# A hybrid diffusion step on one core: the first layer's v split into bf16 halves during the mixer, its expert output in three bf16 passes

## What is computed

```python
def _peer(x, w_q, sub_keys, u, v):
    ...
    best, pos = lax.top_k(cand, PEER_TOPK)
    eidx = jnp.take_along_axis(cidx, pos, axis=-1)
    gate = jax.nn.softmax(best, axis=-1)
    ...
    def block(args):
        xb, ib, gb = args
        hb = jax.nn.gelu(jnp.einsum('tkd,td->tk', u[ib], xb), approximate=False)
        return jnp.einsum('tk,tkd->td', gb * hb, v[ib])
```

## Time and profile before

| | us |
|---|---|
| median of 3 runs | 4829.14 (4827.85 to 4833.03) |
| the profiled execution | 4834.75, its span 4833.2 |
| PE busy | 4347.5 (90%) |
| DVE busy | 3212.7 (66%) |
| ACT busy | 1013.2 (21%) |
| POOL busy | 720.5 (15%) |
| DMA | 1101.75 MB, mean 228 GB/s |

### The profile page before, as it was taken

One profiled execution on the slowest core, in us unless ns is written; L12 is line 12 of the kernel. 1 busy time (PEld: TensorE's weight loads), 2 busy tenths in 40 slices (PEclk: granted clock), 3 DMA queues, 4 the chain that ended last, 5 costly groups with the idle time before them and its releaser, 6 DMA issues. The chain is left out here.

```text
span 4833.2 us, 54964 instructions
## 1 busy us (share of the span) xinstructions
PE 4347.5 (90%) x19374; PEld 2496.9 (52%) x19374; DVE 3212.7 (66%) x6400; ACT 1013.2 (21%) x1581; POOL 720.5 (15%) x548
## 2 busy tenths in 40 slices
PE   8999998978979989999998877987878998999998
PEld 5767674645545545544444555554444554444443
DVE  1666642679978767765653675469997886766664
ACT  2111101122224431100001253213333441100000
POOL 0000000002221113232210000001221112332220
PEclk9999999989989999999999999999998999999999
DMA  4111131149877779999992000116776779999995
GB/s 146 39 39 44 37 133 55 55 182 350 324 278 267 294 275 375 370 385 394 384 360 70 31 1 31 47 50 242 282 284 234 284 272 353 364 397 400 400 396 196
DMA packets 291813, 1101.75 MB, mean 228 GB/s; under 512 B 30704, under 2 KB 131184, under 8 KB 222576
## 3 DMA queue, kind: packets, MB, share of 16 engines
q0 software_dynamic: 74752, 539.00, 28.3%
q1 hardware_dynamic: 185136, 470.64, 27.2%
q10 hardware_dynamic: 31680, 88.88, 4.8%
HBM read 1005.61 MB, written 92.80 MB: 227 GB/s over the span
## 5 line engine op out<-in xcount | busy, mean ns | idle before, releaser
L774 POOL DMA_INDIRECT room_p<-in_uv,ga_eidx_p x512 | 702.8, 1373 | 3309.5 <-DVEq L801 2105.0
L1324 PE MATMUL ex_psF_p<-ex_vst_p,ex_gh_p 128*128 128x512 f32 x1920 | 851.5, 599 | 34.3 <-DVE ex_gh_p L1405 18.1
L800 DVE SCALAR_TENSOR_TENSOR ga_acc_p<-room_p,ga_gw_p,ga_acc_p 128x1024 f32<-128x1024 f32 x504 | 625.1, 1282 | 21.8 <-issue 1.7
L1324 PEld LDWEIGHTS ex_psF_p<-ex_vst_p,ex_gh_p 128*128 128x128 f32 x1920 | 365.9, 192 | 482.5 <-issue 460.6
L786 DVE CUSTOM_DVE_ANT_0 room_p<-room_p,hx_p 128x1024 f32<-128x1024 f32 x512 | 605.5, 1220 | 4.0 <-issue 4.0
L891 PE MATMUL eh_psH_sl_p<-h_hi_p,eh_uhi_sl_p 128*128 128x384 bf16 x1056 | 367.6, 348 | 160.0 <-DVE eh_ulo_sl_p L855 159.9
L1324 PE MATMUL ex_psF_p<-ex_ust_p,ex_gh_p 128*128 128x512 f32 x1152 | 502.1, 593 | 6.6 <-DVE ex_gh_p L1405 6.5
L1405 DVE TENSOR_TENSOR ex_gh_p<-ex_est_p,ex_gst_p 128x384 f32<-128x384 f32 x196 | 107.3, 558 | 397.7 <-DMA ex_est_p<-hidden 253.3
L891 PE MATMUL eh_psH_sl_p<-h_lo_p,eh_uhi_sl_p 128*128 128x384 bf16 x1056 | 366.3, 347 | 0.0
L1324 PEld LDWEIGHTS ex_psF_p<-ex_ust_p,ex_gh_p 128*128 128x128 f32 x1152 | 217.7, 190 | 286.6 <-issue 285.4
L891 PE MATMUL eh_psH_sl_p<-h_hi_p,eh_ulo_sl_p 128*128 128x384 bf16 x1056 | 365.4, 346 | 0.0
(11 more groups left out here) (248 smaller groups left out, 6275.5 us busy)
## 6 DMA issues: line engine op xcount, KB each, us to landing
ex_vst_p<-in_uv SPq DMA_DIRECT2D x160, 512.0 KB, 8.4
eh_ust_sl_p<-in_uT SPq DMA_DIRECT2D x132, 512.0 KB, 5.4
gates<-gt_gs_p ACTq DMA_DIRECT2D x24, 2048.0 KB, 8.0
ex_gst_p<-gates SPq DMA_DIRECT2D x128, 384.0 KB, 13.0
ex_ust_p<-in_uv SPq DMA_DIRECT2D x96, 512.0 KB, 9.3
ex_est_p<-hidden SPq DMA_DIRECT2D x196, 192.0 KB, 10.2
eh_ust_gt_p<-in_uT SPq DMA_DIRECT2D x64, 512.0 KB, 6.6
ex_ust_p<-in_uT SPq DMA_DIRECT2D x60, 512.0 KB, 8.8
```

What stands on the lines that cost most here:

```text
L774: self.nc.gpsimd.indirect_dma_start(self.slot[s % self.RING], None, self.uv, bass.IndirectOffsetOnAxis(self.eidx[:, s:s + 1], 0)).then_inc ...
L800: nc.vector.scalar_tensor_tensor(acc[:], row, self.gw[:, s:s + 1], acc[:], op0=ALU.mult, op1=ALU.add)
L1324: last = nc.tensor.matmul(psF[:, t, x, :], gh[n % 3][:, P * t:P * t + P], vbuf[vslot[n]][:, BANK * x:BANK * x + BANK], start=(n == 0), sto ...
```

## The change

During the first layer's mixer, v of all 128 steps is brought in, split and written back: POOL fetches 128 rows x 1024 fp32 (512 KB) into one of two slots, ACT rounds them to bf16 (`high`), DVE subtracts (`low`) to get the bf16 remainder, and POOL stores both halves (512 KB) to a DRAM tensor `halves`. There are 16 such tiles in each of the 8 heads; the two slots of raw rows and of halves are handed back through POOL. In the expert stage of the first layer v is then loaded from `halves`, as many bytes as before, and `output` makes three bf16 passes, high·high, low·high and high·low, of 6 matmuls each. The gated values are split for it: ACT rounds gh(n), DVE subtracts, in the early steps in the same step, behind u's low half, in the later ones a step behind. gh(n) now waits for the split of gh(n-3), and four buffers of halves wait for the output. The second layer's expert stage is untouched. Two tensors of 2 partitions share one buffer to make room.

```diff
@@ rec_mixer
+            def fetch(h, j):
+                pool.dma_start(vraw[j % 2][:], rows_in[h, j, :, D:2 * D]).then_inc(v_in[j % 2], 16)
+            def stored(h, j):
+                pool.wait_ge(v_out[j % 2], 16 * (VSPLIT // 2 * h + j // 2) + 16)
+                pool.sem_inc(v_free, 1)
+            def split_rows(h, nxt):
+                for j in range(VSPLIT):
+                    pool.wait_ge(v_low, VSPLIT * h + j + 1)
+                    pool.dma_start(halves[h, j], vhl[j % 2][:]).then_inc(v_out[j % 2], 16)
+                    if j + 2 < VSPLIT:
+                        fetch(h, j + 2)
+                    elif nxt is not None:
+                        fetch(nxt, j + 2 - VSPLIT)
+                    if j > 0:
+                        stored(h, j - 1)
+                stored(h, VSPLIT - 1)
             load(0)
+            fetch(0, 0)
+            fetch(0, 1)
             with pool.Fori(1, RH) as h:
+                split_rows(h - 1, h)
                 store(h - 1)
...
+            def high(h, js):
+                for j in js:
+                    act.wait_ge(v_in[j % 2], 16 * (VSPLIT // 2 * h + j // 2) + 16)
+                    act.wait_ge(v_free, VSPLIT * h + j + 1)
+                    nc.scalar.activation(vhl[j % 2][:, 0, :], vraw[j % 2][:], ACT.Copy).then_inc(v_high, 1)
...
-                evacuate(h, s, [Q_, FF_, FB_, G_])
+                for n in (Q_, FF_, FB_, G_):
+                    high(h - 1, range(VSPLIT * n // 4, VSPLIT * (n + 1) // 4))
+                    evacuate(h, s, [n])
...
             for g in range(later.groups):
+                high(RH - 1, range(VSPLIT * g // later.groups, VSPLIT * (g + 1) // later.groups))
...
+            def low(h, n):
+                for j in range(VSPLIT * (n - 1) // 16, VSPLIT * n // 16):
+                    dve.wait_ge(v_high, VSPLIT * h + j + 1)
+                    nc.vector.tensor_tensor(vhl[j % 2][:, 1, :], vraw[j % 2][:], vhl[j % 2][:, 0, :],
+                                            ALU.subtract).then_inc(v_low, 1)
...
                     build(h, s, n)
                     take(h, n - 1)
+                    low(h, n)
...
                 for d in range(2):
+                    low(h, 15 + d)
                     n = TR0 + d
@@ peer_experts
+                    sp.dma_start(vbuf[vslot[n]].bitcast(BF16), halves[n]).then_inc(v_in[vslot[n]], 16)
...
+                for t in range(ND):
+                    tok = slice(P * t, P * t + P)
+                    for j, (g, v0) in enumerate(((g_hi[n % GH], 0), (g_hi[n % GH], D), (g_lo[n % GH], 0))):
+                        for x in range(2):
+                            last = nc.tensor.matmul(psF[:, t, x, :], g[:, tok], both[:, v0 + BANK * x:v0 + BANK * x + BANK],
+                                                    start=(n == 0 and j == 0), stop=(n == NK - 1 and j == 2))
...
             for n in range(NK):
+                if halves is not None:
+                    high(n)
                 gelu(n + 1)
                 take_u(n + 3)
...
                 if n >= 3:
-                    dve.wait_ge(added, n - 2)
+                    dve.wait_ge(added if halves is None else g_low, n - 2)
...
                 take_u(n + 3)
+                while halves is not None and lows < (n + 1 if n < late or n == NK - 1 else n):
+                    low(lows)
+                    lows += 1
                 while gather.paired < begun + paired(n):
```

More of the change, by code:

```diff
@@ L222, in rec_mixer @@
         adab = sb("rec_adab", [P, NMOD * KD, 2])
-        rows = [sb(f"rec_rows{i}", [2, 2, BANK]) for i in range(2)]
+        rows = sb("rec_rows", [2, 2, BANK])
         wst = sb("rec_wst", [P, 5, KD, P])
@@ L239, in rec_mixer @@
         osq = sb("rec_osq", [P, T])
+        vraw = [sb(f"rec_vraw{i}", [P, D]) for i in range(2)]
+        vhl = [sb(f"rec_vhl{i}", [P, 2, D], BF16) for i in range(2)]
+        v_in = [sem(f"rec_v_in{i}") for i in range(2)]
+        v_out = [sem(f"rec_v_out{i}") for i in range(2)]
+        v_high, v_low, v_free = sem("rec_v_high"), sem("rec_v_low"), sem("rec_v_free")
         psA = [ctx.enter_context(nc.psum_tensor(f"rec_psA{s}", [P, 2 * BANK], F32)) for s in range(2)]
@@ L322, in _ @@
                 load(h)
+            split_rows(RH - 1, None)
             store(RH - 1)
@@ L1218, in _, with peer_experts @@
                 sp.wait_ge(sv[s], 16 * (NBL // 2))
-def peer_experts(nc, cst, modT, uT, uv, gates, hid, gather, late, h_hi, h_lo, tag):
+def peer_experts(nc, cst, modT, uT, uv, halves, gates, hid, gather, late, h_hi, h_lo, tag):
     J, TB = 8, 32
@@ L1235, in peer_experts @@
         ge = [sb(f"ex_ge{s}", [P, TD]) for s in range(2)]
+        GH = 4 if halves is not None else 3
         gh = [sb(f"ex_gh{s}", [P, TD]) for s in range(3)]
+        if halves is not None:
+            g_hi = [sb(f"ex_ghi{s}", [P, TD], BF16) for s in range(GH)]
+            g_lo = [sb(f"ex_glo{s}", [P, TD], BF16) for s in range(GH)]
+            g_high, g_low = sem("ex_g_high"), sem("ex_g_low")
         psH = ctx.enter_context(nc.psum_tensor("ex_psH" + tag, [P, 2, BANK], F32))
@@ L1293, in v @@
                     sp.wait_ge(added, vlast[n] + 1)
-                sp.dma_start(vbuf[vslot[n]], uv[P * n:P * n + P, D:2 * D]).then_inc(v_in[vslot[n]], 16)
+                if halves is not None:
+                    sp.dma_start(vbuf[vslot[n]].bitcast(BF16), halves[n]).then_inc(v_in[vslot[n]], 16)
+                else:
+                    sp.dma_start(vbuf[vslot[n]], uv[P * n:P * n + P, D:2 * D]).then_inc(v_in[vslot[n]], 16)
             for n in range(3):
@@ L1317, in hidden, with output_halves @@
                 hidden_products(nc, psH[:, n % 2, 0:TD], u_hi[n % 3], u_lo[n % 3], h_hi, h_lo).then_inc(made, 1)
+            def output_halves(n):
+                pe.wait_ge(v_in[vslot[n]], 16 * vturn[n] + 16)
+                pe.wait_ge(g_low, n + 1)
+                both = vbuf[vslot[n]].bitcast(BF16)
+                for t in range(ND):
[4 more added lines that the diff above has]
+                                                    start=(n == 0 and j == 0), stop=(n == NK - 1 and j == 2))
+                last.then_inc(added, 1)
             def output(n):
+                if halves is not None:
+                    return output_halves(n)
                 pe.wait_ge(v_in[vslot[n]], 16 * vturn[n] + 16)
@@ L1374, in _, with high @@
             gelu(0)
+            def high(n):
+                act.wait_ge(gated, n + 1)
+                if n >= GH:
+                    act.wait_ge(added, n - GH + 1)
+                nc.scalar.activation(g_hi[n % GH][:], gh[n % 3][:], ACT.Copy).then_inc(g_high, 1)
             for n in range(NK):
+                if halves is not None:
+                    high(n)
                 gelu(n + 1)
@@ L1389, in take_u, with low @@
                 nc.vector.tensor_tensor(u_lo[n % 3][:], ust[n % 3][:], u_hi[n % 3][:], ALU.subtract).then_inc(u_low, 1)
+            def low(n):
+                dve.wait_ge(g_high, n + 1)
+                nc.vector.tensor_tensor(g_lo[n % GH][:], gh[n % 3][:], g_hi[n % GH][:], ALU.subtract).then_inc(g_low, 1)
             for n in range(3):
                 take_u(n)
+            lows = 0
             for n in range(NK):
@@ L1422, in _, with peer @@
             dve.drain()
-def peer(nc, cst, modT, wqk, uT, uv, gates, hid, tag, ada=None):
+def peer(nc, cst, modT, wqk, uT, uv, halves, gates, hid, tag, ada=None):
     tiles, pairs = (60, (2, 2, 3)) if ada else (72, (2, 1, 3))
@@ L1440, in peer @@
         peer_gates(nc, cst, pk, gates, gather, (uT, h_hi, h_lo, hid, late + tiles), tag)
-        peer_experts(nc, cst, modT, uT, uv, gates, hid, gather, late, h_hi, h_lo, tag)
+        peer_experts(nc, cst, modT, uT, uv, halves, gates, hid, gather, late, h_hi, h_lo, tag)
 NQ, NKV = AH * HD // P, AKV * HD // P
@@ L1845, in _ @@
             runs(dve, one)
+VSPLIT = 16
 class Const:
@@ L1865, in program @@
         cst.normw = normw[0]
+        halves = nc.dram_tensor("halves", [RH, VSPLIT, P, 2, D], BF16, kind="Internal").ap()
+        by_block = halves.rearrange("h j p e d -> (h j) p (e d)")
         with ExitStack() as c1:
```

14 lines of the change are left out of this document (8 added, 6 removed).

## The result

The changed kernel takes 5006.76 us (median of 4 runs, 5001.51 to 5010.98), the kernel before 4830.32 in the same comparison: a ratio of 1.0365, interval 1.0347 to 1.0383. That is +176 us, where +52 was forecast and 4955 was the upper end of the range. The profiled execution took 5007.12 us (span 5005.6).

The account below looks back on a forecast made before the run. PE was taken to pace the mixer, PE and DMA nearly equally the expert stage. Mixer +82 and expert stage -30 gave +52 on the profiled 4834.75, 4886.75 us; the median lying 5.6 lower, 4881, range 4838 to 4955.

Parts of the forecast that it names:

- Step 1: Mixer levels: DVE's 128 subtractions lie on the path, 10 us a head, 70 us over seven heads.
- Steps 2 and 4: Last head of mixer: PE pieces waited for, 10 us; start: 1 MB of v fetched beside first weights, 2 us.
- Step 3: Mixer, POOL's queue and two-slot ring: 3.9 us a level, narrowly hidden under DVE's 3.93, so no cost.
- Rival B: Mixer: the ring binds, POOL's fetch landing in 6 us, levels 4.6 us, 73 us more, 4954 us; chance 0.14.
- Rival C: Mixer: DVE's copies hold up POOL's issues, 4.39 us between splits, 52 us more, 4933 us; chance 0.10.
- Step 5: First layer's expert stage: three bf16 passes gain 30 us (late 12, tail 15.5, early 3), bounds 5 and 45.
- the bound of -16: Early expert steps: lower bound of their gain, with u landing 3.3 us later, 9.5 us a step.
- Rivals D and E: D: expert transfers follow PE, 4751 us, chance 0.06; E: mixer's DVE idle time takes the splits, 4833 us, chance 0.15.

Follow-up runs that it names:

- the run without transfers: Against the kernel before: all 128 splits on the same two tiles, fetched once, no other fetches, no stores, experts of before; 4919.2 us, ratio 1.0182.
- small stores: Changed kernel's ring with whole 512 KB fetches, stores cut to 128 of 1024 columns, experts of before; 4966.8 us, 1.0276 to the kernel before.
- The small transfers: Changed kernel's two-slot ring, each fetch and store cut to 128 of 1024 columns, experts of before; 4953.6 us, 1.0263 to the kernel before.

## Why the prediction was wrong

Its sign and its stages were right; two terms failed.

**Step 1, DVE's splits: right.** 10 us a head were forecast, 8.8 measured where only the work was there; seven heads 61 for 70. In the levels alone it was 10.7 (mean of the seven heads), for the 10.8 of the working; 2 us came back behind them. The subtraction took 1.226 us and the copy 1.055.

**Steps 2 and 4, last head and start: right in kind.** 14.5 us instead of 10 and 3 instead of 2, both from the run without transfers. The terms then make 79, and 9 us more lie behind the last head's levels, which the steps did not speak of: 87.8 us in that run, for a sum of 82.

**Step 3, POOL's queue and the ring: this step failed.** It said "3.9 us, just not binding". Three things were off, each by little: the landing was 5.3 us, not 4.6; POOL started 0.69 us after DVE's release, not 0.30; and a single value stood for landings that vary. With the measured inputs its own formula gives (0.69 + 0.58 + 5.3 + 1.06 + 1.22) / 2 = 4.4 us a level, 0.5 over DVE's pace; the rest of the way to the 4.6 measured (64.8 / 14) lies in part with the late landings, whose mean is 5.5 us. A hidden term of 3.88 beside a pace of 3.93 left a margin of 0.05 us, on a landing that no row of before showed. The term was put at nothing and measured 93 us. The landing was off in its base and not in the store's share: 4.2 us with small stores where 3.3 was taken from SyncE's queue, and 1.1 for the store where 1.3 was taken.
The Trainium skill's formula (DMA: Bandwidth & Descriptors, "Anatomy of one DMA — SWDGE (gpsimd) path"), an estimate of 3.2 us for 512 KB, is not borne out by these fetches, beside other transfers as they were: with small stores the median was 4.2 and the fastest took 3.7. For 64 KB it gives an estimate of 2.15, and 2.3 was measured.

The 0.30 us was not a wrong reading either. The last head's 16 stores, which stand behind the loop over the heads, still come 0.30 us after the subtraction; the 112 inside the loop come after 0.67 to 0.72, and only they have two more instructions of POOL's sequencer ahead of the issue (in the changed kernel: minimum, median and maximum in ns, first and last start in us):

```profile
L332 POOLq FUSED_REGOPS  x112: 37/37/48, 122.1 to 772.2; - x112
L332 POOLq MOVE halves<-rec_vhl x112: 29/29/38, 122.2 to 772.2; - x112
```

That these set the difference was not tested.

**Rival B was this mechanism.** It named the place, and 4.6 us a level as its result, which came, with a landing of 5.3 where it had asked for 6; its chance of 0.14 was too low for terms so near to each other, and its price of 73 us lacked the end of the head: the 16th split delays kt, and PE's state products wait 4.4 us for it. Of the ring's 12.7 us a head (96.5 - 83.8) 7.1 lie in the levels and 5.6 behind them.

**Rival C did not occur.** POOL's issues beside DVE's copies took 0.53 and 0.54 us, and the 0.69 us ahead of them stayed the same from round to round, behind POOL's own subtractions too. The small transfers showed the opposite, a DVE copy that is 0.1 us longer beside POOL's issues.

**Step 5, the bf16 passes.** The late part and the end gained 21.1 us, for 27.5 forecast (12 and 15.5), at 394 GB/s where 397 was taken; against the 520 to 522 us of the fp32 products behind a mixer that splits, it would be 26 to 28. The early steps were to gain 3 and lost 16.8. The working had put u's low half ahead of the gate's and had counted u's landing; it had not counted that ACT does two things ahead of u, the gates' rounding and the gelu, nor that DVE's 5 us of gather close the round. The loss equals the bound of -16 by chance: u's transfer, which was to cause it, was early. Rounding u first gave the stage 30.7 us, the 30 that step 5 had forecast, but in other shares: 10.4 early and 20.2 later, for 3 and 27.5.

**The sum.** With the measured terms: 87.8 (work) + 92.8 (ring) - 21.1 + 16.8 = 176.3. The medians differ by 176.4; that it fits so closely is chance, since the terms come from single traces whose spans differ by 172.4. Rivals D and E are out: the stage's transfers reached 394 GB/s in the late window (single windows of 25 us up to 413), far from 442, and of DVE's 15.9 us more work in a head's levels (51.28 - 35.43) its idle time took 6.9, while the levels grew by 9.0.
